# One inference step of a hybrid decoder trunk: products with the high part first, and the heads of two mixers in pairs

## The chip, the cores and the metric

One Trainium2 chip, of which the kernel uses one core. The metric is the device time of one execution in microseconds, lower is better. The kernel before was timed in three runs: 1768.33, 1770.8 and 1771.23 us, median 1770.8 us.

## What is computed

The reference runs a trunk of two layers over 256 prompt tokens and, with the same weights, over 8 sequences of 4 new tokens each (32 more), so every matrix product has 288 token columns. Each layer is half a SwiGLU block, a pair of mixers, and half a SwiGLU block; each of them is `x + c * rmsnorm(f(rmsnorm(x)))`. Layer 0 mixes by sparse attention beside an RWKV-7 recurrence, layer 1 by retention beside an mLSTM matrix memory. The parts that the change touches:

```python
def rwkv_step(S, inp):                      # layer 0, 8 heads of 64
    sa = jnp.einsum('bhij,bhj->bhi', S, a_t)
    S = S * w_t[:, :, None, :] + sa[..., None] * b_t[:, :, None, :] + v_t[..., None] * k_t[:, :, None, :]
    return S, jnp.einsum('bhij,bhj->bhi', S, r_t)

def retention_chunk(S, inp):                # layer 1, 4 heads, keys of 64, values of 128
    scores = jnp.einsum('bjhd,bshd->bhjs', q, k) * dmask[None]
    intra = jnp.einsum('bhjs,bshe->bjhe', scores, v)
    inter = jnp.einsum('bjhd,bhde->bjhe', q, S) * jnp.exp((j[:, None] + 1.0) * lg[None, :])[None, :, :, None]

def mlstm_chunk(state, inp):                # layer 1, 4 heads, keys of 64, values of 128
    A = jnp.exp(D - m_j[:, :, None, :]) * jnp.einsum('bjhd,bshd->bjsh', q, k)
    num = jnp.einsum('bjsh,bshe->bjhe', A, v) + sc[..., None] * jnp.einsum('bjhd,bhed->bjhe', q, C)
    den = jnp.sum(A, axis=2) + sc * jnp.einsum('bjhd,bhd->bjh', q, n)
    h = num / jnp.maximum(jnp.abs(den), jnp.exp(-m_j))[..., None]
```

## The kernel before, in words

**Stages.** The program is one sequence of stages on five engines: start, SwiGLU 0, projection into the mixers of layer 0, attention, RWKV, projection out; SwiGLU 1 and 2, projection in of layer 1, its two mixers, projection out, SwiGLU 3. Each engine has its own instruction list, written in the order of the code; semaphores (`wait_ge`, `then_inc`) are all that orders one engine against another, and an engine executes its list in order. So the order in the code is the order on the engine.

**Dense stages.** Activations lie feature-major: `c.x` is 8 tiles of 128 features by 288 tokens. Every f32 product of a weight tile and an activation tile is made as three products of rounded parts (`three_products`, L183 to L187): high weight by high activation (L185), high weight by low activation (L186), low weight by high activation (L187). VectorE makes the two parts of the weights from a 1 MB block (a pair of column tiles, `split_pair`, L171 and L180); ScalarE makes the high part of the activations, `x_hi` (L262), and VectorE the low part, `x_lo` (L276), which needs the high one.

**The start of a dense stage.** The tail of the stage before (`Tail`) ends with a sum on TensorE, then 24 products whose result nobody reads (L325), while VectorE and ScalarE form the new `x` and its two parts tile by tile. `first_two_pairs` then runs the first two weight pairs side by side: tile k of both pairs, 12 products, behind a wait for `x_hi` and `x_lo` of tile k. In SwiGLU 0 alone the two pairs run one after the other. After them comes the sum for the norm (L296), from which VectorE gets `rstd`, reads out the first results and splits weight pair 3.

**RWKV scan (L1186 to L1223).** Five chunks, one after the other. Eight heads lie as four tiles (`h`) by two partition halves (`q`), so a product of one half uses 64 rows and 64 columns of the array, or 128 rows and 64 columns. Per chunk TensorE makes state by a (L1192), the solve (L1203, read out by ScalarE), the state update (L1212, read out by VectorE) and the output y (L1218 from this chunk, L1220 or, in the last chunk, L1222 from the state before). The y part goes head by head.

**The mixers of layer 1 (from L2097).** Four heads; head h has its 64 key rows in partition half h % 2 of tile h // 2. In this order TensorE makes the retention scores (L2102 to L2104), the mLSTM decay exponents (L2117 to L2123), the retention output with eight products of four columns for the eight sequences (L2131 to L2136), sums for the state (L2143, L2153), the mLSTM scores (L2164 to L2166), small broadcasts (L2170 to L2182), the mLSTM numerator and denominator (L2195 to L2201, banks 0 and 1 for an even head, 2 and 3 for an odd one), and the new state and norms (L2206 to L2240). Each block goes head by head; a head's banks are used again two heads later, behind a wait for the read-out (`a_done` by L1989 and L1990 on VectorE, `h_done` by L2013 to L2016 on VectorE). All of these products are plain f32: one product in the code stands in the trace as two weight loads and two matmuls.

## Time and profile before

| | |
|---|---|
| median of 3 runs | 1770.8 us |
| the profiled execution, and its span | 1776.05 us, 1774.2 us |
| TensorE busy (matmuls) | 1578.7 us, 89% |
| VectorE, ScalarE, GpSimd busy | 65%, 18%, 17% |
| mean granted clock of TensorE | 0.893 of full speed |
| TensorE idle before L185, for `ring_r` and for `x_lo_r` | 47.2 us in 10 waits, 18.2 us in 11 waits |
| RWKV scan | about 684 to 729 us |
| mixers of layer 1 | about 1343 to 1500 us |

The span is the time from the first to the last instruction; the execution's own time lies 1.85 us above it. The timeline prints start and duration in us, engine, line, operation, the names written and read, then rows * columns of the array and the operand's shape, then how many such instructions follow each other; in brackets the idle time before and what ended it. The duration of a matmul runs to the end of its results, so the pitch from one start to the next says more than the duration.

### The profile page before, as it was taken

The page shows a single profiled execution, that of the slowest core. Times are in us where ns is not written, and L with a number is a line of the kernel's source. Part 1 is how long each engine was busy: PE and PEld are TensorE (multiplying, and loading weights), DVE is VectorE, ACT ScalarE, POOL GpSimd, SP SyncE. Part 2 cuts the span into 40 slices and gives each one's busy share as a digit, 9 for nine tenths or more (in the row PEclk, how much of TensorE's full clock was granted, in tenths as well). Part 3 has the DMA queues.
Part 4 walks back from the last instruction along what each step waited for, and adds up shares of the span by engine and source line. Part 5 has one row for each costly group of instructions (what it writes and reads, how often), then busy time and mean ns, then how long its engine had stood idle before and what let it go on. Part 6 is the DMA issues. An engine that isn't in the chain of part 4 may idle for free. (4 is left out here: it accounts for less than half of the span.)

```text
span 1774.2 us, 28239 instructions
## 1 busy us (share of the span) xinstructions
PE 1578.7 (89%) x11288; PEld 1394.1 (79%) x11288; DVE 1158.4 (65%) x1396; ACT 311.8 (18%) x599; POOL 308.3 (17%) x270
## 2 busy tenths in 40 slices
PE   6999999976677589779999989999898997899997
PEld 6999989932232377468999989999875684899997
DVE  7876866468871642478876688766746136787764
ACT  2111010032120421122111121111101202221110
POOL 3332110000000000024332143321100000333310
PEclk9999999988779687689999999999997556899999
DMA  6443526336553000054444534443421002544332
GB/s 263 166 165 111 204 81 221 126 131 201 179 182 127 26 2 2 27 196 179 165 142 166 191 119 166 142 161 130 147 95 73 6 22 78 204 144 164 119 131 92
DMA packets 62962, 232.77 MB, mean 131 GB/s; under 512 B 9271, under 2 KB 19164, under 8 KB 45716
## 3 DMA queue, kind: packets, MB, share of 16 engines
q1 hardware_dynamic: 51578, 225.81, 36.0%
q10 hardware_dynamic: 11290, 5.63, 1.1%
q8 instruction: 68, 1.11, 0.3%
q14 instruction: 26, 0.21, 0.0%
HBM read 225.31 MB, written 6.10 MB: 130 GB/s over the span
## 5 line engine op out<-in xcount | busy, mean ns | idle before, releaser
L185 PE MATMUL psum<-x_hi_r,pair_hi 128*128 128x288 f32 x1936 | 579.8, 299 | 65.4 <-DVE ring_r L180 47.2
L187 PE MATMUL psum<-x_hi_r,ring_r 128*128 128x288 f32 x1936 | 577.4, 298 | 0.0
L186 PE MATMUL psum<-x_lo_r,pair_hi 128*128 128x288 f32 x1808 | 537.0, 297 | 0.0
L185 PEld LDWEIGHTS psum<-x_hi_r,pair_hi 128*128 128x128 f32 x1936 | 369.9, 191 | 71.6 <-DVE ring_r L180 39.2
L187 PEld LDWEIGHTS psum<-x_hi_r,ring_r 128*128 128x128 f32 x1936 | 369.0, 191 | 0.0
L186 PEld LDWEIGHTS psum<-x_lo_r,pair_hi 128*128 128x128 f32 x1808 | 344.2, 190 | 0.4
L180 DVE TENSOR_TENSOR ring_r<-ring,pair_hi 128x2048 fp32r<-128x2048 f32 x127 | 327.0, 2575 | 4.3
L185 PE MATMUL psum<-hidden_hi_r,down_hi 128*128 128x288 f32 x704 | 208.4, 296 | 0.0
L186 PE MATMUL psum<-hidden_r,down_hi 128*128 128x288 f32 x704 | 207.7, 295 | 0.0
L187 PE MATMUL psum<-hidden_hi_r,down_r 128*128 128x288 f32 x704 | 207.0, 294 | 0.0
L171 DVE CAST pair_hi<-ring 128x2048 fp32r<-128x2048 f32 x127 | 159.8, 1259 | 35.4 <-DMA ring<-in_w_gu 17.3
L605 POOL TENSOR_TENSOR hidden<-silu,up 128x288 f32 x88 | 128.9, 1464 | 149.4 <-ACT silu L534 147.7
L187 PEld LDWEIGHTS psum<-hidden_hi_r,down_r 128*128 128x128 f32 x704 | 132.6, 188 | 0.0
L186 PEld LDWEIGHTS psum<-hidden_r,down_hi 128*128 128x128 f32 x704 | 132.2, 188 | 0.0
L185 PEld LDWEIGHTS psum<-hidden_hi_r,down_hi 128*128 128x128 f32 x704 | 131.9, 187 | 0.0
L180 DVE TENSOR_TENSOR down_r<-down,down_hi 128x1408 fp32r<-128x1408 f32 x64 | 117.1, 1830 | 2.2
L534 ACT ACTIVATE silu<-gate 128x288 f32<-128x288 f32 x88 | 39.2, 445 | 422.9 <-DVE gate L549 422.9
L180 POOL TENSOR_TENSOR hidden_r<-hidden,hidden_hi_r x88 | 74.3, 844 | 212.3 <-DVE hidden_hi_r L171 212.3
L549 DVE TENSOR_TENSOR gate<-psum,rstd 128x288 f32<-128x288 f32 x88 | 40.1, 456 | 92.5 <-PE psum L187 92.4
L171 DVE CAST down_hi<-down 128x1408 fp32r<-128x1408 f32 x64 | 61.5, 960 | 49.4 <-PE psum L187 30.2
L613 POOL TENSOR_TENSOR ysq<-ysq,y 128x288 f32<-128x288 f32 x24 | 30.7, 1278 | 180.8 <-ACT y L540 180.8
L540 ACT ACTIVATE y<-psum 128x288 f32<-128x288 f32 x32 | 13.2, 412 | 249.2 <-PE psum L187 249.2
(490 smaller groups left out, 1843.8 us busy)
## 6 DMA issues: line engine op xcount, KB each, us to landing
ring<-in_w_gu SPq DMA_DIRECT2D x88, 1024.0 KB, 4.8
down<-in_w_down SPq DMA_DIRECT2D x64, 704.0 KB, 4.2
ring<-in_w_ab SPq DMA_DIRECT2D x18, 1024.0 KB, 5.2
ring<-in_w_cd SPq DMA_DIRECT2D x13, 1024.0 KB, 5.2
ring<-in_cache_k SPq DMA_DIRECT2D x32, 256.0 KB, 4.2
index_keys<-in_cache_k SPq DMA_DIRECT2D x32, 256.0 KB, 4.2
index_keys<-in_cache_i ACTq DMA_DIRECT2D x64, 64.0 KB, 2.7
eight_pages_ds<-in_cache_v SPq DMA_DIRECT2D x16, 256.0 KB, 4.2
```

Of the source, the lines that this page charges most:

```text
L171: return dve.tensor_copy(hi, a)
L180: return eng.tensor_tensor(lo, a, hi.bitcast(F32), ALU.subtract)
L185: pe.matmul(out, w_hi, x_hi, start=start, stop=False)
L186: pe.matmul(out, w_hi, x_lo, start=False, stop=False)
L187: return pe.matmul(out, w_lo, x_hi, start=False, stop=stop)
L534: act.activation(silu[:, b], gate[:, b], ACT.Silu).then_inc(silu_done, 1)
L540: act.activation(y2[:, n % 2], c.banks[4 + n % 2][:, 0:NT], ACT.Square).then_inc(y_squared, 1)
L549: dve.tensor_tensor(gate[:, b], c.banks[bank][:, 0:NT], c.rstd[:, :], ALU.mult).then_inc(gate_scaled, 1)
L605: pool.tensor_tensor(h, silu[:, b], up[:, b], ALU.mult).then_inc(c.hidden_raw, 1)
L613: pool.tensor_tensor(ysq[:, :], ysq[:, :], y2[:, n % 2], ALU.add).then_inc(ysq_added, 1)
```

## The change

At the start of a stage, a tile's eight products with `x_hi` now stand ahead of its four with `x_lo`, and each group has its own wait. In the scan, the y part first makes all products of the chunk (L1218), then all of the state. In the mixers, the two heads of a tile are interleaved product by product, and products of the same number of rows stand together; waits are for two heads at a time. No product is added or left out.

```diff
@@ first_two_pairs
-        tile_ready(k)
-        pair_tile(0, k)
-        if side_by_side:
-            if k == 0:
-                pe.wait_ge(c.pair_split, first + 2)
-            pair_tile(1, k)
+    def tiles(us, k):
+        pe.wait_ge(c.xhi_made, KT * pre + k + 1)
+        for u in us:
+            if k == 0:
+                pe.wait_ge(c.pair_split, first + u + 1)
+            for half in range(2):
+                products_of_high(u, half, k)
+        pe.wait_ge(c.xlo_made, KT * pre + k + 1)
+        for u in us:
+            for half in range(2):
+                mm = product_of_low(u, half, k)
@@ the scan, y part
-                for h in range(HP):
-                    for q in range(2):
-                        mm = pe.matmul(B[2][half(q), h * n:h * n + n], U[:, c_, q, h], G[:, c_, q, h, L:L + n], start=True, stop=(c_ == 0))
-                        if 0 < c_ < 4:
-                            mm = pe.matmul(B[2][half(q), h * n:h * n + n], ST[half(q), (c_ - 1) % 2, h], AR[half(q), 1, h, c_ * L:c_ * L + L], start=False, stop=True)
+                for h, q in heads:
+                    mm = pe.matmul(B[2][half(q), h * n:h * n + n], U[:, c_, q, h], G[:, c_, q, h, L:L + n], start=(h == 0), stop=(c_ == 0), skip_group_check=True)
+                for h, q in heads:
+                    if 0 < c_ < 4:
+                        mm = pe.matmul(B[2][half(q), h * n:h * n + n], ST[half(q), (c_ - 1) % 2, h], AR[half(q), 1, h, c_ * L:c_ * L + L], start=False, stop=True, skip_group_check=True)
@@ retention scores; the mLSTM scores in the same way, with one wait for a_done 2
+            for hp in range(2):
+                for o, w, s0, n in BLOCKS:
+                    for p_ in range(2):
+                        mm = pe.matmul(B[2 * hp + p_][0:n, o:o + w], K[half(p_), hp, s0:s0 + n], Q[half(p_), hp, s0:s0 + w], start=True, stop=True)
@@ decay exponents
-                for o, w, s0, j0 in ((0, TP, 0, 0), (TP, P, P, P)):
-                    pe.matmul(bk[:, o:o + w], gu[:, s0:s0 + P], sel_row(h)[:, 0:w], start=True, stop=False)
-                    pe.matmul(bk[:, o:o + w], sel[:, h], negM[:, j0:j0 + w], start=False, stop=False)
-                    pe.matmul(bk[:, o:o + w], c.ident[:, :], lmask[:, 0:w], start=False, stop=True)
+                for o, w, s0 in two:
+                    pe.matmul(bk[:, o:o + w], gu[:, s0:s0 + P], sel_row(h)[:, 0:w], start=(o == 0), stop=False, **sg_)
+                for o, w, s0 in two:
+                    pe.matmul(bk[:, o:o + w], sel[:, h], negM[:, s0:s0 + w], start=False, stop=False, **sg_)
+                for o, w, s0 in two:
+                    pe.matmul(bk[:, o:o + w], c.ident[:, :], lmask[:, 0:w], start=False, stop=True, **sg_)
@@ mLSTM numerator and denominator; the retention output in the same way, without a wait for h_done
-            for h in range(4):
-                if h >= 2:
-                    pe.wait_ge(S["h_done"], h - 1)
+            for hp in range(2):
+                two = (2 * hp, 2 * hp + 1)
+                if hp:
+                    pe.wait_ge(S["h_done"], 2)
+                for h, bn, l0, l1, l2 in sides:
                     pe.matmul(B[bn][:, 0:TP], l0, scT[:, 4 + h, 0:TP], start=True, stop=False, **sg_)
                     pe.matmul(B[bn][:, P:TP], l1, scT[:, 4 + h, TP:ST_COLS], start=False, stop=True, **sg_)
+                for h, bn, l0, l1, l2 in sides:
                     pe.matmul(B[bn][:, TP:NT], l2, scs[:, 4 + h], start=False, stop=False, **sg_)
                 for b in range(NB):
+                    for h in two:
+                        pe.matmul(B[2 * (h % 2)][:, o:o + TS], c0t[half(h % 2), b, hp], qsc[half(h % 2), hp, b * TS:b * TS + TS], start=False, stop=True, **sg_)
+                for h in two:
+                    pe.matmul(B[2 * (h % 2) + 1][:, TP:NT], c.ones[half(h % 2), :], qn[half(h % 2), hp], start=False, stop=True, **sg_).then_inc(S["num_sum"], 1)
```

TensorE's list at the start of SwiGLU 2, before: behind the 24 unread products, each tile's products go high, low, high.

```order
L325 MATMUL psum<-hidden_hi_r,down_hi_7284 128x288 x24
L185 MATMUL psum<-x_hi_r,pair_hi 128x288
L186 MATMUL psum<-x_lo_r,pair_hi 128x288
L187 MATMUL psum<-x_hi_r,ring_r 128x288
L185 MATMUL psum<-x_hi_r,pair_hi 128x288
L186 MATMUL psum<-x_lo_r,pair_hi 128x288
L187 MATMUL psum<-x_hi_r,ring_r 128x288
```

The same place in the changed kernel (lines 229, 230 and 234 are its L185, L187 and L186):

```order
L334 MATMUL psum<-hidden_hi_r,down_hi_7300 128x288 x24
L229 MATMUL psum<-x_hi_r,pair_hi 128x288
L230 MATMUL psum<-x_hi_r,ring_r 128x288
L229 MATMUL psum<-x_hi_r,pair_hi 128x288
L230 MATMUL psum<-x_hi_r,ring_r 128x288
L229 MATMUL psum<-x_hi_r,pair_hi 128x288
L230 MATMUL psum<-x_hi_r,ring_r 128x288
L229 MATMUL psum<-x_hi_r,pair_hi 128x288
L230 MATMUL psum<-x_hi_r,ring_r 128x288
L234 MATMUL psum<-x_lo_r,pair_hi 128x288 x4
```

The four products that read `x_lo` moved behind the eight that don't. TensorE's list in the second chunk of the scan, before (`U_rk` is the solve's result, `ST_rk` the state, `x_hi` holds the right-hand sides here):

```order
L1203 MATMUL psum<-x_hi 64x64 x8
L1212 MATMUL psum<-U_rk,ring 64x64 x8
L1218 MATMUL psum<-down,U_rk 64x64
L1220 MATMUL psum<-ring,ST_rk 64x64
L1218 MATMUL psum<-down,U_rk 64x64
L1220 MATMUL psum<-ring,ST_rk 64x64
L1218 MATMUL psum<-down,U_rk 64x64
L1220 MATMUL psum<-ring,ST_rk 64x64
```

And in the changed kernel, where L1212, L1221, L1227 and L1230 are those four lines and L1201 is L1192:

```order
L1212 MATMUL psum<-x_hi 64x64 x8
L1221 MATMUL psum<-U_rk,ring 64x64 x8
L1227 MATMUL psum<-down,U_rk 64x64 x8
L1230 MATMUL psum<-ring,ST_rk 64x64 x8
L1201 MATMUL psum<-ST_rk,ring 64x64 x8
```

Sixteen alternating products became two runs of eight. TensorE's list for the mLSTM numerator and denominator of the first head, before (`down` and `scs_cm` are the scores, `vtok` the values, `ring` the cached state):

```order
L2195 MATMUL psum<-down,vtok_7296 128x256
L2196 MATMUL psum<-down,vtok_7296 128x128
L2197 MATMUL psum<-scs_cm,vtok_7296 128x32
L2195 MATMUL psum<-down,ones 128x256
L2196 MATMUL psum<-down,ones 128x128
L2197 MATMUL psum<-scs_cm,ones 128x32
L2200 MATMUL psum<-qsc_cm,ring 128x4 x8
L2201 MATMUL psum<-qn_cm,ones 128x32
```

And of the first two heads in the changed kernel, from the last of its eight large products on:

```order
L2216 MATMUL psum<-down,ones 128x128
L2218 MATMUL psum<-scs_cm,vtok_7312 128x32
L2218 MATMUL psum<-scs_cm,ones 128x32
L2218 MATMUL psum<-scs_cm,vtok_7312 128x32
L2218 MATMUL psum<-scs_cm,ones 128x32
L2222 MATMUL psum<-qsc_cm,ring 128x4 x16
L2224 MATMUL psum<-qn_cm,ones 128x32 x2
```

The small products of two heads now stand together, those of L2222 and L2224 alternating between the two partition halves.

## Rows read from the trace of the kernel before

**Rows 1.** The page's first part: busy time, share, instructions.

```profile
PE 1578.7 (89%) x11288; PEld 1394.1 (79%) x11288; DVE 1158.4 (65%) x1396; ACT 311.8 (18%) x599; POOL 308.3 (17%) x270
```

**Rows 2.** Timeline of TensorE at the start of SwiGLU 2.

```profile
1023.03 0.37 PE L185 MATMUL psum<-x_hi_r,pair_hi 128*128 128x288 f32 x1 [2.49 <-DVE x_lo_r L276]
...
1028.33 0.37 PE L185 MATMUL psum<-x_hi_r,pair_hi 128*128 128x288 f32 x1 [1.09 <-DVE x_lo_r L276]
...
1038.01 0.65 PE L296 MATMUL psum<-sqsum_ffn,ones 128*128 128x288 f32 x2
...
1046.68 0.40 PE L185 MATMUL psum<-x_hi_r,pair_hi 128*128 128x288 f32 x1 [1.64 <-DVE ring_r L180]
```

**Rows 3.** Timeline of ScalarE and VectorE there: x_hi of tile 0, x_lo of tiles 2 and 3.

```profile
1020.96 0.53 ACT L262 ACTIVATE x_hi_r<-x,gains 128x288 fp32r<-128x288 f32 x1 [3.08 <-DVE x L362]
...
1027.14 2.02 DVE L276 SCALAR_TENSOR_TENSOR x_lo_r<-x,gains,x_hi_r 128x288 fp32r<-128x288 f32 x2
```

**Rows 4.** Timeline of TensorE in the RWKV scan.

```profile
686.01 1.07 PE L1218 MATMUL psum<-down,U_rk 128*64 128x64 f32 x16
687.01 1.12 PE L1192 MATMUL psum<-ST_rk,ring 64*64 64x64 f32 x16
...
691.54 0.42 PE L1218 MATMUL psum<-down,U_rk 128*64 128x64 f32 x2
691.89 0.47 PE L1220 MATMUL psum<-ring,ST_rk 64*64 64x64 f32 x2
...
697.71 1.16 PE L1192 MATMUL psum<-ST_rk,ring 64*64 64x64 f32 x15
...
723.47 0.42 PE L1218 MATMUL psum<-down,U_rk 128*64 128x32 f32 x2 [0.87 <-ACT U_rk L1057]
...
729.08 3.45 PE L1229 MATMUL psum<-z,ring 128*64 128x512 f32 x8
```

**Rows 5.** Busy time of L1385 (scores in attention, halves alternating) in a stretch.

```profile
369.79:373.76 3.97, 3.97 (x18) 3.54 (x20) 0.50 0.51 161
```

**Rows 6.** Timeline of TensorE: four-quadrant products of eight columns before the scan.

```profile
679.82 3.90 PE L1182 MATMUL psum<-ring,s0t_rk 64*64 64x8 f32 x128
```

**Rows 7.** Timeline of TensorE in the mixers of layer 1.

```profile
1350.70 1.22 PE L2102 MATMUL psum<-z 64*128 64x256 f32 x2 [4.83 <-DVE z L1916]
...
1357.96 1.54 PE L2108 MATMUL psum<-ident,z 128*128 128x128 f32 x6
1359.43 1.22 PE L2117 MATMUL psum<-sel_cm,g_cm 4*128 4x256 f32 x2
...
1364.91 1.22 PE L2117 MATMUL psum<-sel_cm,g_cm 4*128 4x256 f32 x2
...
1381.35 1.22 PE L2131 MATMUL psum<-down,vtok 128*128 128x256 f32 x2
...
1386.99 1.22 PE L2131 MATMUL psum<-down,vtok 128*128 128x256 f32 x2
...
1416.92 1.22 PE L2164 MATMUL psum<-qk_cm 64*128 64x256 f32 x2
...
1431.63 1.06 PE L2195 MATMUL psum<-down,vtok 128*128 128x256 f32 x2
...
1439.72 1.22 PE L2195 MATMUL psum<-down,vtok 128*128 128x256 f32 x2
```

**Rows 8.** Instructions grouped by line and shape: the four-column products of the retention output.

```profile
L2136 PE MATMUL psum<-qdec_cm,ring 64*128 64x4 f32 x64 | 14.3, 352 | 0.0
```

**Rows 9.** Timeline of VectorE: mLSTM scores of one head, then read-out of head 0.

```profile
1418.92 0.56 DVE L1989 SCALAR_TENSOR_TENSOR down<-psum,down 128x384 f32<-128x384 f32 x1 [0.48 <-PE psum L2166]
...
1439.83 0.46 DVE L2013 SCALAR_TENSOR_TENSOR hd_cm<-psum,emj_cm 128x288 f32<-128x288 f32 x1 [6.81 <-PE psum L2201]
...
1442.80 0.46 DVE L2016 TENSOR_TENSOR x_hi<-psum,hr_cm 128x288 f32<-128x288 f32 x1
```

**Rows 10.** Stretches: busy time per engine, granted clock, DMA share, GB/s.

```profile
1350.00:1480.00 130.00, 125.11 (x430) 92.04 (x430) 51.57 (x130) 15.14 (x38) 0.00 (x0) 0.50 0.06 23
1480.30:1485.90 5.60, 5.60 (x18) 3.95 (x18) 4.57 (x11) 3.00 (x8) 0.00 (x0) 0.75 0.46 189
```

More of the change, by code:

```diff
@@ L224, in first_two_pairs, with products_of_high, product_of_low @@
 def first_two_pairs(c, pe, first, pre, side_by_side):
-    def tile_ready(k):
-        pe.wait_ge(c.xhi_made, KT * pre + k + 1)
-        pe.wait_ge(c.xlo_made, KT * pre + k + 1)
-    def pair_tile(u, k):
-        for half in range(2):
-            mm = pair_products(c, pe, c.banks[4 - 2 * u + half], first, u, half, k)
-        if k == KT - 1:
-            mm.then_inc(c.pair_done, 1)
-    pe.wait_ge(c.pair_split, first + 1)
-    for k in range(KT):
-        tile_ready(k)
-        pair_tile(0, k)
-        if side_by_side:
-            if k == 0:
-                pe.wait_ge(c.pair_split, first + 2)
-            pair_tile(1, k)
-    if not side_by_side:
-        pe.wait_ge(c.pair_split, first + 2)
-        for k in range(KT):
-            pair_tile(1, k)
+    def products_of_high(u, half, k):
+        s = (first + u) % RING
+        out = c.banks[4 - 2 * u + half][:, 0:NT]
+        pe.matmul(out, c.whi[:, s, half, k], c.xhi[:, k], start=(k == 0), stop=False)
+        pe.matmul(out, c.ring_lo[:, s, half, k], c.xhi[:, k], start=False, stop=False)
+    def product_of_low(u, half, k):
+        s = (first + u) % RING
+        return pe.matmul(c.banks[4 - 2 * u + half][:, 0:NT], c.whi[:, s, half, k], c.xlo[:, k], start=False, stop=(k == KT - 1))
+    def tiles(us, k):
+        pe.wait_ge(c.xhi_made, KT * pre + k + 1)
+        for u in us:
[3 more added lines that the diff above has]
+                products_of_high(u, half, k)
+        pe.wait_ge(c.xlo_made, KT * pre + k + 1)
+        for u in us:
+            for half in range(2):
+                mm = product_of_low(u, half, k)
+            if k == KT - 1:
+                mm.then_inc(c.pair_done, 1)
+    if side_by_side:
+        for k in range(KT):
+            tiles((0, 1), k)
+    else:
+        for u in range(2):
+            for k in range(KT):
+                tiles((u,), k)
 class Pre:
@@ L2115, in _ @@
                 bk = B[6 + h % 2]
[L2116 to L2119 removed]
+                two = ((0, TP, 0), (TP, P, P))
+                for o, w, s0 in two:
+                    pe.matmul(bk[:, o:o + w], gu[:, s0:s0 + P], sel_row(h)[:, 0:w], start=(o == 0), stop=False, **sg_)
@@ L2134, in _ @@
                 for b in range(NB):
                     o = TP + b * TS
-                    mm = pe.matmul(B[h][:, o:o + TS], rs0[hf, b, hp], qdec[hf, hp, b * TS:b * TS + TS], start=False, stop=True, **sg_)
-                mm.then_inc(S["y_sum"], 1)
+                    for h in two:
+                        mm = pe.matmul(B[h][:, o:o + TS], rs0[half(h % 2), b, hp], qdec[half(h % 2), hp, b * TS:b * TS + TS], start=False, stop=True, **sg_)
+                mm.then_inc(S["y_sum"], 2)
             pe.wait_ge(S["kt_out"], 1)
@@ L2158, in _ @@
             pe.wait_ge(S["rp_out"], 1)
[L2159 to L2166 removed]
+            for hp in range(2):
+                if hp:
+                    pe.wait_ge(S["a_done"], 2)
+                for o, w, s0, n in BLOCKS:
+                    for p_ in range(2):
+                        mm = pe.matmul(B[4 + p_][0:n, o:o + w], qk[half(p_), 2 + hp, s0:s0 + n], qk[half(p_), hp, s0:s0 + w], start=True, stop=True)
+                        if s0 == TP:
+                            mm.then_inc(S["qk_sum"], 1)
             pe.wait_ge(S["rn_out"], 4)
```

56 lines of the change are left out of this document (24 added, 32 removed).

## The prediction

> **What bounds the kernel now.** I read the page's first part, then the granted clock in stretches, then TensorE's timeline where it waits or runs slowly, then the other engines at those places. The first part shows TensorE busy 89% of the span [rows 1]. So the bound is TensorE, and a change of order can pay in two ways: fewer idle gaps, or products that take less time each. The places are three.
>
> At the start of a dense stage TensorE waits for `x_lo` [rows 2]: 2.49 us before tile 0, and 1.09 us before tile 2 at 1028.33. From there it runs to the sum at 1038.01 without a gap: 72 products in 9.68 us, 0.134 us each.
>
> In the scan every product of y costs more than the same product does alone. Sixteen L1218 in a row stand 1.00 us (686.01 to 687.01). In the next chunk L1218 and L1220 alternate, and 32 of them stand from 691.54 to 697.71, 6.17 us [rows 4]: 0.19 us each instead of 0.06. Alternating between 128 rows and 64 rows costs both the overlap of the two halves and a gap.
>
> The mixers of layer 1 run at clock 0.50 for all of 1350 to 1480, with TensorE busy 125 of 130 us [rows 10]. They are bound by TensorE at the lower of its two levels, 1.2 GHz. Here half of the array idles: one head's keys use 64 rows.
>
> **What a pair of halves costs.** The nearest row is L1385, the attention's scores, where products alternate between partition halves at the same shape (64 * 128, 256 columns) and the same clock: 18 matmuls in 3.97 us, 0.22 us each [rows 5]. In the mixers a head's three score products take 1.81 us, as 1350.70 to 1357.96 holds four heads [rows 7]; its two matmuls of 256 columns fill about 1.0 us of that. So two halves run beside each other and the second is free. For products of four columns the weight load is what counts: 64 matmuls of L2136 are busy 14.3 us, 0.22 us each [rows 8]. Whether two such loads overlap is not shown for halves of full width. For quadrants it is: 128 matmuls in 3.75 us, 0.03 us each at full clock, about half of what a load of 64 columns alone would take (0.22 us at half the clock for 128 columns makes 0.055 us) [rows 6]. Bounds for the pair: free (as there) or double (no overlap). I take free.
>
> **The change, part by part** (savings against the profiled execution, 1776.05 us).
>
> *Stage starts.* At the last wait, `x_lo` of tile 2 (1028.2, the first of the two in that row [rows 3]), eight of the tile's twelve products are now done. TensorE can begin at about 1021.6, after `x_hi` of tile 0 at 1021.5 [rows 3]; it then waits again for each of the three `x_lo` and has time for it. Behind the last wait stand 64 products instead of 72: 8 x 0.134 = 1.07 us. The sum at 1038.01, `rstd` and the split of pair 3 (the 1.64 us wait [rows 2]) all follow from the end of these products and move with them. Five such starts: 5.3 us. SwiGLU 0 gains nothing: it waits for the weights. The new wait for `x_lo` has only these four products and the next tile behind it. Bounds: 0 (clock colder) to 8.
>
> *Scan.* y becomes 16 L1218 in 1.00 us and 16 L1220 of the shape of L1192, again about 1.0 us: 2.0 instead of 6.17, 4.2 us saved, in three chunks 12.6. In the last chunk y takes 5.61 us (723.47 to 729.08 [rows 4]) and becomes about 2.1, saving 3.5. The state update on VectorE lies beside y and takes under 1.2 us after L1212, so y and the next L1192 stay back to back. Sum 16.1. Bounds: 13 to 18.
>
> *Retention scores.* 7.26 us for four heads become two pairs of 1.81: 3.6 saved.
>
> *Decay exponents.* A head takes 5.48 us (1359.43 to 1364.91). Its streams at 0.44 us per 256 columns (18 matmuls over two halves in 3.97 us) are 3.9 us of large products and 0.3 of small ones; the remaining 1.3 us are five changes of row count, 0.26 each. Two of the five go: 0.55 per head, 2.2 in all.
>
> *Retention output.* A head takes 5.64 us (1381.35 to 1386.99), 3.5 of it four-column products. A pair takes 3.5 once, and two changes of row count less: 11.3 becomes 7.3; 7.9 saved in two pairs. If weight loads do not overlap, 7.0 of it is lost.
>
> *mLSTM scores.* The block that begins at 1416.92 has the twelve products of the retention scores, so 7.26 us become 3.6; but the second pair needs both banks, so it waits for two read-outs of some 0.65 us (0.56 for L1989 and a small one) [rows 9]: 1.6 us of new wait. 2.0 saved.
>
> *Numerator and denominator.* A head takes 8.2 us (the row at 1431.63 is already under way, 8.09 to 1439.72). A pair takes the four-column products once (3.5 less), L2201 once (0.5 less), and four changes of row count less (1.1): 16.4 becomes 11.3. Here the change adds its largest wait: `h_done` 2 instead of 1. VectorE reads one head out in 3.43 us (1439.83 to 1443.26 [rows 9]); both sums of a pair come at its end, so TensorE stands 2 x 3.43 + 0.1 = 7.0 us. Before, it read out head 1 beside head 2 and nothing waited. Behind the last pair the read-out of two heads, 6.9 us, lies beside L2206 to L2214. Net 2 x 5.1 - 7.0 = 3.2 saved.
>
> The Trainium skill speaks against this block: TensorEngine Tiling (Array Packing), PSUM Bottleneck, warns that row tiling speeds up TensorE but not the reading of PSUM, and advises to divide that between ScalarE and VectorE. ScalarE takes no part in this read-out. By the rule the sum has the 7.0 us; without it the sum would be 7.0 larger. The trace has the 3.43 us, and I follow it.
>
> *Clock.* Behind 1480.3 stand sixteen dense products of 288 columns, and the clock, 0.50 until there, has a mean of 0.75 over their first 5.6 us [rows 10]: it rose halfway through. In the block of numerator and denominator before, large products come two at a time (1.6 us) between small ones, and it stays at 0.50. Now eight stand in a row, 5.3 us. I expect the clock to rise in each pair after some 3 to 5 us and the rest of the pair, some 7 us at half clock, to take half: 3.4 us twice, 6.8. Bounds: 0 to 10.
>
> By the Trainium skill (TensorE: Matmul & The Clock Gate, HAM oscillation) idle stretches bring the clock back to 1.2 GHz; the 7.0 us wait would be one, so the second pair begins slow. The sum has it so; if the clock held, it would be about 3 us larger.
>
> **Sum:** 5.3 + 16.1 + 3.6 + 2.2 + 7.9 + 2.0 + 3.2 + 6.8 = 47.1 us: 1776.05 becomes 1729. The median of the runs shown, 1770.8, lies 5.25 us below the profiled execution, so the forecast is 1770.8 - 47.1 = 1723.7 us.
>
> **Rivals.**
>
> *The clock stays low in the mixers* (everything else as above): 40.3 us, 1730.5. For it: 125 us of busy TensorE did not raise it [rows 10]. Against it: it rose at once under dense products.
>
> *The clock rises in more places.* In the scan a chunk becomes 3.9 us of unbroken work out of 6.5. If it rises there too, products of two or three chunks halve, 2 us each, and some of the retention output's: 6 us more, 1718.
>
> *Weight loads of two halves do not overlap.* Then the four-column products of both blocks, 4 pairs x 3.5, and L2201 save nothing: 15 us less, 1739. For it: no row shows the case itself. Against it: the quadrants.
>
> *Slower: each change of partition half costs a gap,* as the change between 128 and 64 rows does in the scan, where a product takes 0.39 us in alternation (6.17 / 16) against 0.21 for its two matmuls alone. The new lists change half some 90 times in the mixers; at 0.26 us a change that is 23 us, halves no longer overlap (3.6, 7.0 and 8.0 us are lost and the mLSTM scores give 3.6 less), the new waits of 1.6 and 7.0 us stay, and the clock does not rise. The 47.1 become 47.1 - 6.8 - 22.2 - 23 = -5: 1776 us. It decides from about 0.2 us a change. Against it: L1385 changes half every four matmuls at 0.22 us each, with no such gap.
>
> *The new order does nothing at the starts* because `x_lo` of tile 2 sets the end either way: it does, but the eight products are behind it before and ahead of it after. Price 5.3: 1729.
>
> **How the numbers follow.** Forecast 44%; clock low in the mixers 26%; clock high in more places 14%; loads not overlapping 8%; nothing at the starts 4%; slower 2%; else 2%. The range 1711 to 1738 reaches from the high-clock case with the upper bounds of scan and starts (1718 less 7) to just short of the case without overlap of loads. 0.2%, 3.5 us, is about what the measurement can tell from no change. Faster by more 97%, within 1%, slower 2%.
>
> **What would show it.** In the profile after: at each start the first product with `x_hi` some 1.4 us earlier and the last wait for `x_lo` ahead of four products, 1.07 us from sum to sum; 16 L1218 and 16 L1220 in about 2 us per chunk, chunks of 6.5 instead of 10.7 us; retention scores in 3.6 us; four-column products of a pair at 0.11 us each; a wait of about 7 us for `h_done` and one of 1.6 for `a_done`; the clock at 1.00 inside the numerator block. The forecast is wrong if the four-column products keep 0.22 us, if a gap stands at each change of half, or if the stretch from 1350 to 1480 shrinks by less than 12 us.

## The result

The changed kernel takes 1713.3 us, median of 4 runs (1708.53 to 1716.6), against 1771.01 (1768.33 to 1776.85) before: ratio 0.9668, 95% interval 0.9633 to 0.9703, so 57.7 us less. Forecast were 1723.7 us in a range of 1711 to 1738, so 47.1 less. In its profiled execution it takes 1715.16 us, 60.9 less than the profiled one of before. Executions of one and the same kernel differ by some 8 us, so medians are compared by their intervals and traces stretch by stretch.

The first part of its page, to be read against [rows 1]:

```profile
PE 1516.6 (89%) x11288; PEld 1346.1 (79%) x11288; DVE 1158.1 (68%) x1396; ACT 311.5 (18%) x599; POOL 304.1 (18%) x270
```

TensorE executes the same 11288 matmuls and is busy 62.1 us less; its share stays 89% since the span shrank with it. The other engines' busy time has hardly moved.

TensorE's timeline at the start of SwiGLU 2 after the change (beside [rows 2]):

```profile
996.36 0.40 PE L229 MATMUL psum<-x_hi_r,pair_hi 128*128 128x288 f32 x1 [1.01 <-ACT x_hi_r L271]
...
1000.13 0.81 PE L234 MATMUL psum<-x_lo_r,pair_hi 128*128 128x288 f32 x4 [0.53 <-DVE x_lo_r L285]
...
1003.05 0.80 PE L234 MATMUL psum<-x_lo_r,pair_hi 128*128 128x288 f32 x4 [1.04 <-DVE x_lo_r L285]
...
1011.68 0.65 PE L305 MATMUL psum<-sqsum_ffn,ones 128*128 128x288 f32 x2
```

The last wait for `x_lo` is as long as before (1.04 us; it was 1.09), but only 64 products stand between it and the sum, 8.63 us instead of 9.68.

TensorE's timeline in the scan (beside [rows 4]):

```profile
686.05 1.07 PE L1227 MATMUL psum<-down,U_rk 128*64 128x64 f32 x16
...
688.69 0.68 PE L1212 MATMUL psum<-x_hi 64*64 64x64 f32 x16 [0.52 <-DVE x_hi L958]
690.24 0.68 PE L1221 MATMUL psum<-U_rk,ring 128*64 128x64 f32 x16 [0.87 <-ACT U_rk L1066]
690.75 0.64 PE L1227 MATMUL psum<-down,U_rk 128*64 128x64 f32 x16
691.32 0.68 PE L1230 MATMUL psum<-ring,ST_rk 64*64 64x64 f32 x16
691.91 0.68 PE L1201 MATMUL psum<-ST_rk,ring 64*64 64x64 f32 x16
693.11 0.68 PE L1212 MATMUL psum<-x_hi 64*64 64x64 f32 x16 [0.52 <-DVE x_hi L958]
...
705.31 3.60 PE L1239 MATMUL psum<-z,ring 128*64 128x512 f32 x8
```

A chunk takes 4.42 us (688.69 to 693.11) instead of 10.73, and y 1.16 instead of 6.17. The first chunk runs at half clock (0.50, 1.2 GHz) as before (L1227 in 1.00 us); from 688.69 on every group of sixteen takes little over half of that.

TensorE's timeline in the mixers of layer 1 (beside [rows 7]):

```profile
1323.21 3.66 PE L2114 MATMUL psum<-z 64*128 64x256 f32 x24 [4.83 <-DVE z L1926]
...
1327.95 0.92 PE L2130 MATMUL psum<-sel_cm,g_cm 4*128 4x256 f32 x4 [0.28 <-DVE mnew_cm L1945]
...
1330.92 1.64 PE L2130 MATMUL psum<-sel_cm,g_cm 4*128 4x256 f32 x4
...
1348.39 1.95 PE L2154 MATMUL psum<-qdec_cm,ring 64*128 64x4 f32 x32
...
1353.87 3.58 PE L2154 MATMUL psum<-qdec_cm,ring 64*128 64x4 f32 x32
...
1373.66 1.90 PE L2182 MATMUL psum<-qk_cm 64*128 64x256 f32 x12 [1.37 <-DVE scs_cm L2000]
...
1382.94 1.06 PE L2215 MATMUL psum<-down,vtok 128*128 128x256 f32 x2
...
1396.57 1.22 PE L2215 MATMUL psum<-down,vtok 128*128 128x256 f32 x2 [6.85 <-DVE x_hi L2026]
...
1405.03 3.58 PE L2229 MATMUL psum<-kws_cm,vtok 128*128 128x64 f32 x16
```

Thirty-two four-column matmuls of a pair take 3.58 us, 0.11 each, where sixteen of one head took 3.57; at the upper clock level 1.95. The two new waits are there, 6.85 and 1.37 us. Six stretches of that trace show how the clock moved (columns as in [rows 10]):

```profile
688.00:705.00 17.00, 10.95 (x291) 9.40 (x288) 5.95 (x14) 4.17 (x11) 0.00 (x0) 0.99 0.03 10
1323.20:1330.80 7.60, 7.32 (x48) 5.62 (x48) 7.36 (x30) 0.66 (x3) 0.00 (x0) 0.73 0.41 171
1331.00:1346.00 15.00, 15.00 (x55) 11.79 (x56) 13.51 (x50) 1.98 (x7) 0.00 (x0) 0.50 0.01 4
1347.00:1350.00 3.00, 3.00 (x40) 2.79 (x38) 0.00 (x0) 0.00 (x0) 0.00 (x0) 0.98 0.00 0
1351.00:1385.00 34.00, 28.86 (x130) 19.14 (x129) 9.30 (x22) 10.90 (x23) 0.00 (x0) 0.50 0.09 36
...
1402.00:1405.00 3.00, 3.00 (x44) 2.95 (x44) 0.00 (x0) 0.00 (x0) 0.00 (x0) 1.00 0.00 0
```

In the scan the clock is at 2.4 GHz with TensorE busy 64% of the time. In the exponents, from their second head on (1331.00), it is at 1.2 GHz with TensorE busy all of the time. So in this trace the level does not follow the share of busy time.

### The profile page after: what moved, and what is told of

It is laid out like the page before. It is cut to its first block and busy times, and to the rows that moved or that the text cites. A ratio compares the mean times of both kernels' runs of the same rounds, so it can differ in the third digit from the quotient of the medians.

```text
span 1713.3 us, 28197 instructions
## 1 busy us (share of the span) xinstructions
PE 1516.6 (89%) x11288; PEld 1346.1 (79%) x11288; DVE 1158.1 (68%) x1396; ACT 311.5 (18%) x599; POOL 304.1 (18%) x270
## 5 line engine op out<-in xcount | busy, mean ns | idle before, releaser
L185 PE MATMUL psum<-x_hi_r,pair_hi 128*128 128x288 f32 x1744 | 520.7, 299 | 36.0 <-DVE ring_r L180 36.0
L187 PE MATMUL psum<-x_hi_r,ring_r 128*128 128x288 f32 x1744 | 519.5, 298 | 0.0
L186 PE MATMUL psum<-x_lo_r,pair_hi 128*128 128x288 f32 x1616 | 478.7, 296 | 0.0
L185 PEld LDWEIGHTS psum<-x_hi_r,pair_hi 128*128 128x128 f32 x1744 | 332.4, 191 | 39.5 <-DVE ring_r L180 39.1
L187 PEld LDWEIGHTS psum<-x_hi_r,ring_r 128*128 128x128 f32 x1744 | 331.8, 190 | 0.0
L186 PEld LDWEIGHTS psum<-x_lo_r,pair_hi 128*128 128x128 f32 x1616 | 306.4, 190 | 0.4
L185 PE MATMUL psum<-hidden_hi_r,down_hi 128*128 128x288 f32 x704 | 208.5, 296 | 0.0
L186 PE MATMUL psum<-hidden_r,down_hi 128*128 128x288 f32 x704 | 207.9, 295 | 0.0
L187 PE MATMUL psum<-hidden_hi_r,down_r 128*128 128x288 f32 x704 | 207.2, 294 | 0.0
L187 PEld LDWEIGHTS psum<-hidden_hi_r,down_r 128*128 128x128 f32 x704 | 132.6, 188 | 0.0
L186 PEld LDWEIGHTS psum<-hidden_r,down_hi 128*128 128x128 f32 x704 | 132.2, 188 | 0.0
L185 PEld LDWEIGHTS psum<-hidden_hi_r,down_hi 128*128 128x128 f32 x704 | 132.0, 188 | 0.0
L171 DVE CAST down_hi<-down 128x1408 fp32r<-128x1408 f32 x64 | 62.1, 970 | 49.3 <-PE psum L187 29.0
```

What stands on the lines that cost most here:

```text
L171: return dve.tensor_copy(hi, a)
L185: pe.matmul(out, w_hi, x_hi, start=start, stop=False)
L186: pe.matmul(out, w_hi, x_lo, start=False, stop=False)
L187: return pe.matmul(out, w_lo, x_hi, start=False, stop=stop)
```

## The experiments

Times are medians; ratios are to the kernel before on the same chip, with 95% intervals. "Full change" is the changed kernel. Where stretches of two traces are compared, the mixers are taken from the first score product to the first L2245 (KB products): 122.5 us before (1350.70 to 1473.24), 90.5 with the full change (1323.21 to 1413.70).

### One part of the change at a time

**f1_starts**: the kernel before with the new `first_two_pairs` alone.

> The kernel before with the new order at the stage starts alone. Theory: eight products fewer behind the last wait for x_lo, 1.07 us at each of five starts, so 5.3 us less than before (ratio 0.997), and each start, from the first product to the sum of squares, keeps its end 1.07 us earlier. Rival 1 (x_lo or the ring sets the end anyway): no change, ratio 1.000. Rival 2 (some of what the full change gained elsewhere, 1.7 us in the attention, comes from the starts too): 7 us less, ratio 0.996.

Measured: 1761.44 us, ratio 0.9949 (0.9931 to 0.9968), 9.8 us less by the medians. The interval, 6 to 12 us less, leaves out the theory's 5.3 by a little and holds rival 2's 7. From the first `x_lo` on VectorE to the sum a start takes 14.5 us instead of 15.63 at four places and 14.5 instead of 16.1 at SwiGLU 3, the same five numbers as in the full change: 6.2 us in all. The rest is not in the starts. Two places whose code is as before ran faster in this trace: the numerator block of the mixers took 29.95 us instead of 32.85, since the clock was up for a part of it, and the scan 41.60 instead of 43.07. The scan's second chunk, to be read against [rows 4]:

```profile
690.01 0.69 PE L1221 MATMUL psum<-U_rk,ring 128*64 128x64 f32 x16 [0.87 <-ACT U_rk L1066]
...
690.74 0.33 PE L1229 MATMUL psum<-ring,ST_rk 64*64 64x64 f32 x2
...
691.25 0.33 PE L1229 MATMUL psum<-ring,ST_rk 64*64 64x64 f32 x2
...
692.67 0.47 PE L1229 MATMUL psum<-ring,ST_rk 64*64 64x64 f32 x2
...
693.48 0.47 PE L1229 MATMUL psum<-ring,ST_rk 64*64 64x64 f32 x2
```

The clock was at its upper level when y began; then the alternating products came, a pair of them every 0.51 us (690.74 to 691.25), and within 2 us it had fallen: every 0.81 us (692.67 to 693.48). In the profiled execution of before the clock did not rise there. So two executions of the same code differ by 1.5 us in that chunk alone (9.27 us here, 10.73 there), with no edit to it. The trace of f3_mixers, with the old scan too, shows the same rise and fall.

**f2_scan**: the kernel before with the scan's new order alone.

> The kernel before with the scan's y grouped by shape alone. Theory after seeing the trace of the full change: 16 us from the order at half clock, and 8 more since the unbroken products bring TensorE to its upper level within the second chunk, 24 us less than before (ratio 0.9865), chunks of 4.4 us. Rival 1 (the clock rises in the full change because of something earlier, such as the new starts): clock 0.50 throughout, chunks of 6.5 us, 16 us less (ratio 0.991). Rival 2 (the three parts do not add up, since each speeds up what another also would): the three kernels with one part each save less than 57.7 us together or more.

Measured: 1753.04 us, ratio 0.989 (0.9866 to 0.9914), 18.2 us less by the medians. Its trace has the chunks of 4.43 us of the full change, and from the first L1218 to the products that follow the scan it takes 19.26 us, exactly as there; before it was 43.07. So what comes before the scan is not needed for the upper level (rival 1 falls by the trace, though its ratio of 0.991 lies inside the interval). What the order does is narrower than the text expects: the clock was up at the start of the second chunk in f1_starts and f3_mixers as well, with the old order, and fell once y alternated. The new order keeps it up. It also lets it rise later: f12_full_change_again, the same program as the full change, began its second chunk at half clock and was up from the third on.

```profile
689.44 1.07 PE L1227 MATMUL psum<-down,U_rk 128*64 128x64 f32 x16
...
691.34 1.04 PE L1201 MATMUL psum<-ST_rk,ring 64*64 64x64 f32 x16
692.91 0.68 PE L1212 MATMUL psum<-x_hi 64*64 64x64 f32 x16 [0.53 <-DVE x_hi L958]
```

Eleven traces have y in groups; in eight the clock is up from the second chunk on, in three (f10, f11, f12) from the third, and their scan takes 21.2 us. In the three traces with the old order it is never up behind the second chunk. The lines above also give the order's worth without the clock: y takes 1.90 us at half clock (689.44 to 691.34) instead of 6.17, the chunk 6.37 instead of 10.73. The medians show less than the trace; the scan of before, 43.07, was slower than in the two other traces with the old scan (41.6).

**f3_mixers**: the kernel before with the paired heads alone.

> The kernel before with the paired mixer heads alone. Theory: as in the full change, 31 us less than before (ratio 0.9825): scores 3.6, decay exponents 4.3, retention output 10.8, mLSTM scores 2.1, numerator and denominator 10.8. Rival (the clock rises there only by the luck of where the chip's clock decisions fall after the earlier changes): the terms as forecast without it, 3.6 + 2.2 + 7.9 + 2.0 + 3.2 = 18.9 us (ratio 0.989), with clock 0.50 up to the numerator.

Measured: 1742.48 us, ratio 0.9845 (0.9823 to 0.9868), 28.8 us less; the rival's 0.989 lies outside the interval. The stretch of the mixers takes 91.1 us, as in the full change (90.5). The three parts alone save 9.8 + 18.2 + 28.8 = 56.8 us by the medians, together 57.7: they add up as far as intervals of 3 to 5 us each can tell.

### Why grouping by shape pays in the scan

**f4_scan_groups_4** and **f9_scan_groups_2**: the full change, y in groups of four or of two products.

```
-for h, q in heads: 128-row product
-for h, q in heads: 64-row product
+for g0 in range(0, 8, 4):                    # f9: (0, 8, 2)
+    for h, q in heads[g0:g0 + 4]: 128-row product
+    for h, q in heads[g0:g0 + 4]: 64-row product
```

> The full change, but in the scan y comes in groups of four products with 128 rows and four with 64 rows in turn: 7 changes of row count inside y instead of 1 (before: 31). Theory A (each change of row count costs a fixed gap, (6.17 - 2.0) / 30 = 0.14 us at half clock): y takes 2.0 + 6 x 0.14 = 2.8 us at half clock, three chunks and the last 3.3 us more than the full change if the clock acts alike, up to 11 more if it stays at 0.50 (ratio to before 0.969 to 0.973). Rival B (what cost time was that the two halves did not stand side by side): nothing more, ratio 0.967, y 2.0 us at half or 1.1 at full clock.

> The full change, but the scan's y comes in groups of two products: two with 128 rows, one on each half, then two with 64 rows. Inside y the row count changes 7 times (before 15, groups of four 3, full change 1). Groups of four took 1.37 us at full clock against 1.16, so 0.10 us for each further change. Theory (a gap per change, and the rest of the old cost is the overlap of the two halves, which pairs keep): y takes 1.16 + 6 x 0.10 = 1.8 us at full clock, 2.5 us over the four chunks, 1716 us, ratio to before 0.9685, if the clock rises as in the full change. Rival (the further changes bring the clock down again, as one product at a time did: there y began at the upper level and fell to the lower within 1.5 us): chunks of 6 us or more, 6 to 8 us more than the full change, ratio 0.972.

The first text counts wrongly: a chunk has eight products of each kind (a product is two matmuls), so before the row count changed 15 times inside y, and with groups of four it changes 3 times. Measured: groups of four 1711.4 us, ratio 0.9671 (0.9649 to 0.9693), no difference; groups of two 1721.75, 0.9724 (0.9693 to 0.9755). One chunk's y in the trace of the kernel with groups of four:

```profile
686.77 0.40 PE L1228 MATMUL psum<-down,U_rk 128*64 128x64 f32 x8
...
687.86 0.45 PE L1231 MATMUL psum<-ring,ST_rk 64*64 64x64 f32 x8
688.14 0.63 PE L1201 MATMUL psum<-ST_rk,ring 64*64 64x64 f32 x16
```

and the same in the kernel with groups of two:

```profile
690.81 0.29 PE L1228 MATMUL psum<-down,U_rk 128*64 128x64 f32 x4
...
692.61 0.33 PE L1231 MATMUL psum<-ring,ST_rk 64*64 64x64 f32 x4
692.77 0.63 PE L1201 MATMUL psum<-ST_rk,ring 64*64 64x64 f32 x16
```

All at the upper level, y takes 1.16 us in one block of each shape, 1.37 in fours (2 changes more), 1.96 in twos (6 more): 0.10 to 0.13 us a change. One at a time, at the pace of f1_starts' first products, it would be 8 x 0.51 = 4.1: 14 changes by 0.13 are 1.8 over the 1.16, and the other 1.1 us fits what groups of two keep and single products lose, the two halves side by side; no run separates the two further. By this sum theory A and rival B each hold a part. In groups of two the clock held at its upper level to the end of the scan (1.00 from 688.80 to 708.30), so the rival of f9_scan_groups_2 did not come about; in groups of four it fell in the last half of the last chunk's y (0.58 from 701.30 to 702.40). The chunk in twos is 5.18 us against 4.42, 3 us over the scan. The 8 us between the medians (interval of the ratio +-0.003, so +-5 us) are more than the trace explains.

### Which part of a pair is free

**f5_halves_apart**: the full change, half 0's sixteen four-column matmuls ahead of half 1's.

```
-for b in range(NB):
-    for h in two: matmul(... half(h % 2), b ...)
+for h in two:
+    for b in range(NB): matmul(... half(h % 2), b ...)
```

> The full change, but of a pair of heads the sixteen four-column matmuls on half 0 come first and then the sixteen on half 1 (retention output and numerator). Theory A (two weight loads overlap only where neighbours stand on different halves): 0.22 us each again at half clock and about 0.12 at full, so the retention output costs 3.5 us more in the pair at half clock and 1.8 in the one at full clock, the numerator 1.8 in each pair: 8.9 us more than the full change (1713.3), 1722, ratio to before 0.972. Rival B (loads are taken ahead in any order): no difference, ratio 0.967. Rival C (the longer low-density stretch also brings the clock down in the numerator): up to 6 us more still, ratio 0.976.

Measured: 1723.27 us, ratio 0.9729 (0.9702 to 0.9757). Its two retention output groups, to be read against 1.95 and 3.58 us above, and the two stretches that they stand in (columns as in [rows 10]):

```profile
1345.81 4.16 PE L2154 MATMUL psum<-qdec_cm,ring 64*128 64x4 f32 x32
...
1353.75 6.16 PE L2154 MATMUL psum<-qdec_cm,ring 64*128 64x4 f32 x32
```

```profile
1345.80:1349.90 4.10, 4.10 (x33) 4.08 (x32) 0.00 (x0) 0.00 (x0) 0.00 (x0) 0.78 0.02 4
1353.80:1359.80 6.00, 6.00 (x33) 6.00 (x32) 0.00 (x0) 0.00 (x0) 0.00 (x0) 0.50 0.00 0
```

The second group is the clean comparison: all at half clock, 6.16 us against 3.58, 0.19 a matmul against 0.11, where one head alone has 0.22. Of the first group's extra 2.2 us a part is clock, since its mean was 0.78. The trace of f10_numerator_by_head, below, has the measure at the upper level (1.00 from 1385.65 to 1387.45):

```profile
1385.64 1.95 PE L2218 MATMUL psum<-qsc_cm,ring 64*128 64x4 f32 x16
```

Sixteen such matmuls of one head alone take as long as 32 that alternate. Theory A holds in the main: weight loads of the two halves overlap if they alternate, and apart they take 6.16 of the 7.0 us that two heads take one after the other; why a part of the overlap is left is not shown. It is the order within the pair that pays. The stretch of the mixers is 101.6 us against 90.5, 5.1 more in the retention output and 6.0 in the numerator, where the theory had 3.6. There the clock fell to 0.50 within each group of four-column products; so a part of rival C is there, though its 0.976 lies just outside the interval.

**f10_numerator_by_head**: the full change, numerator and denominator head by head as before.

> The full change without its pairs in the numerator and denominator, where the forecast had a net gain of 3.2 us at equal clock and 6.8 from the clock. Theory: the block takes 32.85 us again instead of 22.09, at clock 0.50: 10.8 us more than the full change, 1724 us, ratio to before 0.973. Rival 1 (the new waits eat the gain and the clock would have risen anyway, since the stretch before it now runs faster): 3 us more, 0.9685. Rival 2 (the wait of 6.85 us costs more than the pairs bring): less time than the full change.

Measured: 1720.81 us, ratio 0.9716 (0.9691 to 0.9741), 7.4 us over the full change on the same chip. The block takes 29.99 us (1381.81 to 1411.80) against 22.09 with pairs and 32.85 before: here the clock rose late in the first head and fell early in the second. So the pairs bring 7.9 us in spite of the wait (6.4 against the trace of f12_full_change_again, whose block takes 23.57), and the other 2.9 us of the 10.8 between before and after are clock that the block can find without any pair in it. f1_starts shows the same: the code of before takes 29.95 us there. Neither the theory's 10.8 nor rival 1's 3 was met; rival 2 falls.

### The new waits, and the clock in the exponents

**f6_banks**: the full change with other banks; the readers and all that follows change banks with it.

```
-if hp: pe.wait_ge(S["h_done"], 2)
+if hp: pe.wait_ge(S["kd_out"], 1)
-sides: banks 2 * (h % 2) and the next
+sides: banks 4 * hp + 2 * (h % 2) and the next   # what follows: bank numbers xor 4
-mLSTM scores, second pair: banks 4, 5, wait a_done 2
+mLSTM scores, second pair: banks 0, 1, wait y_out 4
```

> The full change, but the numerator's second pair writes banks 4 to 7 instead of 0 to 3, what follows it takes the banks of the other four, and the second pair of mLSTM scores writes banks 0 and 1. Theory: the wait for h_done (6.85 us) and the one for a_done (1.37) go, and the second pair stays at the upper clock level (6.7 us instead of 8.5); L2229 waits until 1396.5 for the first pair's read-out instead of starting at 1405.0. 8.5 + 1.4 = 9.9 us less than the full change: 1703, ratio to before 0.961. Rival (VectorE becomes the bound: its four read-outs take 13.7 us and then come the KB products, so the wait moves in front of L2245): 4 us less at most, 1709, ratio 0.965.

Measured: 1708.61 us, ratio 0.9651 (0.9631 to 0.967): about 3 to 5 us less than the full change, where 9.9 were expected. The intervals of the two overlap (the full change has 0.9633 to 0.9703, and again 0.9657 to 0.9702), so this gain rests on the trace. The waits are gone:

```profile
1380.73 1.06 PE L2215 MATMUL psum<-down,vtok 128*128 128x256 f32 x2
...
1388.83 1.22 PE L2215 MATMUL psum<-down,vtok 128*128 128x256 f32 x2
...
1397.53 3.27 PE L2229 MATMUL psum<-kws_cm,vtok 128*128 128x64 f32 x16
```

The block takes 16.8 us instead of 22.09, and the scores up to it 1.4 less. But the second pair takes 8.70 us, since behind the first pair's four-column products the clock is at 1.2 GHz again: the expectation that it would stay up without the wait was wrong. (In f8 and f11, below, the second pair began near the upper level and fell within 1 us.) And in this execution the retention output found the clock low in both pairs (14.7 us against 11.8). The whole stretch is 86.4 us against 90.5. VectorE was not the bound: from the numerator to the KB products TensorE waits for none of its read-outs.

**f7_rows128**: the full change with the exponents' and emj's operands on 128 rows, 124 of them zero.

```
-self.sel = sb("sel", [4, 4, P])      g = sb("g", [4, 9, NT])      negM = sb("negM", [4, NT])
+self.sel = sb("sel", [P, 4, P])      g = sb("g", [P, 9, NT])      negM = sb("negM", [P, NT])
+for t in (gu_all, negM_all[:, :], gem_all): pool.memset(t, 0.0)
```

> The full change, but the decay exponents' products and those of emj run on 128 rows, of which 124 are zero, instead of on 4 (GpSimd writes the zeros once). Columns and count are the same. Theory (in the clock's decision a product of 4 rows counts as little work; the clock fell at 1331 though TensorE was busy without a gap): the clock stays at 1.00 through the exponents, which take about 10 us instead of 17.6, and through the retention output's second pair (4.7 instead of 7.1): 10 us less than the full change, 1703, ratio to before 0.961. Rival A (busy time is what counts, and the fall has another cause): clock 0.50 as before, and only the changes of row count are saved, 1 to 2 us, ratio 0.966. Rival B (VectorE's new wait for the zeros stands in the chain to the scores): 1 us more.

Measured: 1696.6 us, ratio 0.9573 (0.9546 to 0.96). The starts of the second and third head of the exponents, and a stretch from within the first head, where the clock rose, to the start of the retention output's second pair:

```profile
1332.36 0.92 PE L2134 MATMUL psum<-sel_cm,g_cm 128*128 128x256 f32 x4
...
1334.94 0.92 PE L2134 MATMUL psum<-sel_cm,g_cm 128*128 128x256 f32 x4
```

```profile
1330.70:1345.00 14.30, 14.30 (x115) 12.46 (x115) 14.16 (x55) 2.94 (x10) 0.00 (x0) 0.97 0.02 5
```

The same number of matmuls with the same columns, most rows zero, and the clock rises and holds at 2.4 GHz where it had fallen to 1.2. A head takes 2.58 us instead of 4.89; the four 10.9 instead of 17.6. Rival A falls. One rival the text does not name: on 128 rows most changes of row count go too, and in the scan such changes went with the fall. Two things speak against it. With y in groups of two the scan has 7 such changes in a chunk of 5.18 us and stays at 1.00; the first head of the exponents, ahead of the fall, had 4 in 2.97 us, which is no more for its time. And the eight emj matmuls (L2195, here L2199) have no change among them: with 4 rows the first numerator row behind them is still slow, 1.06 us in all seven traces of paired heads; with 128 rows it takes 0.64 to 0.67 in all three. Rival B is there in part: the first score products start 0.48 us later (TensorE's wait ahead of the first score products is 5.31 us instead of 4.83). The retention output's second pair still fell to half clock, so its 2.4 us were not won. The stretch shrinks from 90.5 to 81.6 us, the medians by 16.7; this kernel's runs reach from 1692.2 to 1705.7 and the profiled one is the slowest of them. The trace shows 9 of the 16.7; where the others come from was not seen.

**f8_banks_rows128**: both.

> Both of the two edits before (other banks, and 128 rows). Theory: they act in different blocks, so 9.9 + 10 = 20 us less than the full change: 1693, ratio to before 0.956. Rival (part of one gain is the clock level, which the other already gives back): 14 us less, 1699, ratio 0.959.

Measured: 1694.5 us, ratio 0.9575 (0.9547 to 0.9603): by the runs no better than 128 rows alone, though its stretch is 70.2 us, 11.4 less than there. The interval holds the additive theory and its rival; the trace, with 20.3 us less than the full change, speaks for the former.

**f11_banks_rows128_vb**: the same, and the second pair's VB products go to KB's place ahead of the read-outs, their matmuls to banks 2 and 3.

```
-if hp: dve.wait_ge(S["rn_sum"], 1)          # one buffer for both pairs
+VBs[hp]: VB for the first pair, KB's place for the second
-if hp: pe.wait_ge(S["rn_out"], 2)           # banks 6, 7
+if hp: pe.wait_ge(S["y_out"], 4)            # banks 2, 3
```

> Other banks and 128 rows, and the second pair's VB products of VectorE go to a buffer of their own ahead of the read-out, the matmuls that use them to banks 2 and 3. Theory: the wait of 3.76 us between the two blocks of L2171 goes, 3.8 us less than the kernel with other banks and 128 rows (1694.5): 1691, ratio to before 0.9555; with the idle time gone the clock may hold into the mLSTM scores, 3 us more. Rival (the read-outs of the first pair, 2.8 us of VectorE, then stand before the scores' read-outs): 1 us less at most, 0.957.

**f12_full_change_again** on the same chip:

> The full change once more, beside the last version on the same chip. Theory: 0.967 of before, 1713 us, as measured first, and 16 to 20 us above the version with other banks, 128 rows and VB. Rival (part of the distance of 17 us between the two, where the traces show 9.5 to 20, is the clock of single executions): the distance comes out at 22 or at 12 us.

Measured: 1680.89 us, ratio 0.9496 (0.9472 to 0.9519), and the full change 1713.45, 0.968 (0.9657 to 0.9702). The last version beats both kernels, by 89 and by 33 us. The wait of 3.76 us has gone from between the two groups of L2175 (L2171 before), and more with it:

```profile
1335.94 1.95 PE L2158 MATMUL psum<-qdec_cm,ring 64*128 64x4 f32 x32
...
1339.88 1.95 PE L2158 MATMUL psum<-qdec_cm,ring 64*128 64x4 f32 x32
...
1342.84 3.23 PE L2175 MATMUL psum<-VB_cm,kw_cm 32*64 32x512 f32 x8
1345.85 3.63 PE L2175 MATMUL psum<-KB_cm,kw_cm 32*64 32x512 f32 x8
...
1364.09 1.95 PE L2226 MATMUL psum<-qsc_cm,ring 64*128 64x4 f32 x32
...
1371.70 1.95 PE L2226 MATMUL psum<-qsc_cm,ring 64*128 64x4 f32 x32
```

Here the clock was up for the four-column products of all four pairs (1.95 us each). From the first score product to the KB products it takes 63.6 us, against 90.5. The theory's 3.8 us and the 3 more that it gives to the clock fit the 6.6 by which this stretch is shorter than in f8_banks_rows128, and the rival's 1 us does not. The median lies 13.6 us below f8_banks_rows128. The distance from the full change, 33 us, is larger than both the theory's 16 to 20 and the rival's 22. A part of such distances lies in code that no edit touched: from the attention's scores to the scan (the first four-quadrant products) f11 takes 304.9 us, f8 309.7, and the other traces between 306.5 and 310.6. So some 27 us of the 33 stand in the mixers' rows, and the rest is not credited to the edits.

## Why the prediction was right

The order of products and the pairs did what was forecast; the clock did more than was forecast, and for a reason that was in part another. Each term can be read in the two profiled traces:

| term | forecast, us | in the traces, us |
|---|---|---|
| five stage starts | 5.3 | 6.2 |
| scan, first L1218 to L1229 | 16.1 | 43.07 - 19.26 = 23.8 |
| retention scores | 3.6 | 3.7 |
| decay exponents | 2.2 | 21.9 - 17.6 = 4.3 |
| retention output | 7.9 | 22.6 - 11.8 = 10.8 |
| mLSTM scores | 2.0 | 7.25 - 5.10 = 2.15 |
| numerator and denominator, with clock | 3.2 + 6.8 | 32.85 - 22.09 = 10.8 |
| sum | 47.1 | 61.8 |

The other stretches take back 0.9 us, which makes 60.9; by the medians it is 57.7. Of the 14.7 us between the two sums some 13 are clock: 7.7 in the scan, 2.9 in the retention output, 1.9 in the exponents, 0.8 in the numerator.

That the result lies in the range owes something to luck. The range's low end is given as 1718 less 7 for the upper bounds of scan and starts, but those bounds add 1.9 + 2.7 = 4.6, which makes 1713; the result is 1713.3. The case that came, the clock up in more places, had 14% and 6 us, and it brought about twice that.

**Stage starts.** As worked out: 1.13 us at four of them, where 1.07 was forecast. The fifth, SwiGLU 3, was 0.5 us slower than the others before and is equal to them now. All five are shown by f1_starts alone. There are two waits for `x_lo` left at a start, not three.

**Scan.** The step "y becomes 2.0 us" held: f12_full_change_again has it whole, 1.90 us at half clock. What was mis-sized is the clock. The forecast had it at 0.50 throughout and gave "the clock rises in more places" 14%, with 6 us. f2_scan shows the scan's own order keeping it at the upper level from the second chunk on, worth the 7.7 us between 16.1 and 23.8; where it rises a chunk later, 5.8. That rival's 1718 us lay nearer to the result than the forecast's 1724. f1_starts and f3_mixers show the other side: under alternating products the clock came down from its upper level.

**Pairs.** "The second is free" is right for score products (3.66 us for four heads) and for four-column products (0.11 us each at half clock), the step for which only quadrants spoke. f5_halves_apart shows the condition: the halves must alternate. The 15 us rival, loads that don't overlap, is nearly the kernel that has them in another order, and it costs 10. The retention output brought 2.9 us more than its term because the clock was up for most of its first pair: 4.69 us there and 7.11 in the second, where 7.3 was the forecast for each.

**Exponents.** Two changes of row count less are 0.59 us a head at half clock (5.48 to 4.89; forecast 0.55). The other 1.9 us is the clock: the first head ran mostly at the upper level, in 2.97 us, and then it fell.

**Numerator.** The wait for `h_done` was forecast at 7.0 us and is 6.85. The Trainium skill's warning (TensorEngine Tiling (Array Packing), PSUM Bottleneck) that pairs speed up TensorE and not the read-out is borne out by it. But taking the wait away is worth less than its length: the block of f6_banks is 5.3 us shorter without it, not 8.5. The clock rose earlier than the "3 to 5 us" of the forecast in the first pair, after about 2 us (from 1385.11 on L2215 takes 0.60 us instead of 1.06), and after about 5 us in the second; the gain is some 7 us, as the 6.8 of the forecast. The second pair began slow behind the idle time, as the sum had it; f6_banks shows that it also begins slow without any idle time. So the idle time, which the forecast took for the cause with the Trainium skill's rule (TensorE: Matmul & The Clock Gate, HAM oscillation), was not needed for it: in that trace the clock was down at the end of the busy products just ahead. The total of the block, 10.8 us against 10.0, hides this, and also that the block of before took 2.9 us less in another execution (f1_starts).

**Slower or no change.** No trace has a gap at a change of half: twenty-four score matmuls (twelve products) over two halves stand in 3.66 us.

## What to carry to other kernels

List TensorE's products by shape and by the rows they use: put equal row counts in a block, and let products on the two halves alternate one by one within it. Then look at the granted clock of each stretch beside the busy share: a stretch that is busy all the time can stand at 1.2 GHz and hide as much as a wait does (6.7 us in the exponents, beside a wait of 6.85), and here the same products on 128 rows, filled with zeros, brought the clock back. The waits that the pairing added went by the bank numbers alone, but what that is worth is measured, not read off their length. And before a difference of a few us is put down to an edit, look at the stretches that no edit touched: here they differ by as much.

## What the runs showed of the hardware

A change between 128 and 64 rows costs 0.10 to 0.13 us at the upper clock level (y in groups of four and two). Weight loads of 64 rows overlap in pairs when halves alternate: 0.11 us a matmul against 0.19 with the halves apart and 0.22 for one half alone, all at half clock; 0.06 against 0.12 for one half alone at full clock. Products of 256 columns on 4 rows let the clock fall while TensorE never idled; the same products on 128 rows with zeros held it at 0.97. The same code in the same place can meet either level from one execution to the next, which is 1.5 us in one old scan chunk, 2.0 in a new one and 2.9 in the numerator block. The largest scatter seen is elsewhere, 304.9 to 310.6 us between the attention's scores and the scan; what makes it was not looked into.
